# Every wait of TensorE as an instruction of its own, in a one-core transformer kernel of 14,410 matmuls

## The chip, the cores and the metric

The kernel runs on one core of a Trainium2 chip. The metric is the device time of one execution in microseconds (us). Three runs of the kernel before gave 2484.98, 2485.29 and 2485.33 us, so the median is 2485.29 us. A further execution was recorded by the hardware profiler; it took 2487.22 us, and all rows below come from it.

## The reference, cut to what matters

The program computes two transformer blocks in float32 on one sequence of 512 tokens with 1024 channels, one after the other.

```python
D_MODEL = 1024; SEQ = 512; D_FF = 2816; N_MEM = 256

def first_block(x, mem, ...):
    h = rmsnorm(x, norm_mix_pre)
    x = x + rmsnorm(parallel_mixer(h, ...), norm_mix_post)     # 31-tap conv branch, and 8-head attention
    h = rmsnorm(x, norm_mem_pre)
    x = x + rmsnorm(memory_cross_attention(h, ...), norm_mem_post)   # 4 heads of 256 over 256 memory rows
    h = rmsnorm(x, norm_ffn_pre)
    return x + rmsnorm(conv_gated_ffn(h, ...), norm_ffn_post)

def second_block(x, ...):
    for i in range(2):
        x = x + 0.5 * swiglu(rmsnorm_2(x, ffn1_norm[i]), ...)
        h = rmsnorm_2(x, mix_norm[i])
        x = x + (pool_mixer(h, ...) if i == 0 else mla_mixer(h, ...))
        x = x + 0.5 * swiglu(rmsnorm_2(x, ffn2_norm[i]), ...)
    return x

def swiglu(h, w_gate, w_up, w_down):
    return (silu(h @ w_gate) * (h @ w_up)) @ w_down
```

The matmuls of the five feed-forward parts are most of the work. The float32 result is wanted, so each product of two float32 matrices is made of three products in a shorter format, below.

## The kernel before, in words

All activations lie with their channels on the 128 partitions and the 512 tokens along the row. A weight matrix comes in units, most of them of 1024 rows and 128 columns. For each unit ScalarE writes a rounded copy `wh` (line 542) and VectorE the remainder `wl` (line 551); activations are split in the same way into `hxh` and `hxl` (lines 756 and 764) and other pairs. A product of the two matrices is then three matmuls for each block of 128 rows: high by high and the two mixed ones. They are lines 600, 601 and 602 in the helper `mm3`, and lines 1967 to 1969 in the four feed-forward parts that form sums of weight quarters and work on 256 tokens at a time. A unit of eight blocks is thus 24 matmuls into one PSUM bank, and a quarter unit of four blocks is 12.

In the program each matmul is one instruction, and it becomes two on the engine: a load of its 128 by 128 weights and the matmul proper. The profile shows the first as PEld and the second as PE. 
The order of the work on each engine is written out by hand, in functions with names such as `heads_tensor` or `block_tensor`. The engines meet through semaphores. Every engine has a wrapper class over `Engine`, whose method `wait_ge` (lines 185 to 189) takes a semaphore's name and a value. It does nothing when this engine has already waited for that value or a higher one (the dictionary `seen`), and otherwise issues a wait:

```python
        self.seen[kind] = value
        self.e.wait_ge(self.signals.sems[kind], value)
```

Of these some 650 have one or two waits more ahead of them, which makes 663 EVENT_SEMAPHORE instructions, of which 21 hold two waits. Together these are 1,993 waits.

The typical place is `linear`, which makes one tile of output:

```python
            e.wait_ge(*sig.at(("low", i)))
            for k in range(nk):
                sh, sl, ready = src(k0 + k)
                e.wait_ge(*sig.at(ready))
                made = mm3(e, o, (h[:, k, :], lo[:, k, :]), (sh, sl), first and k == 0, last and k == nk - 1)
```

It waits for the low part of the weight unit, and for each block of activations when that block is new. Its callers wait before that for the PSUM bank to be free. The last matmul of a tile raises `unit_done`.

The stages, by time in the profiled execution: the first block's projections and convolution until about 117 us, its attention (`main<-pt,vh` and `score<-kh,qh`, the latter with 64 active rows) until about 208 us, output projection and norm (about 280 to 305 us), attention over the memory (about 341 to 370 us), then the feed-forward parts, the pooling mixer near 1160 us and the latent attention (about 1900 to 2110 us).

Of the kernel before, what the change touches and what calls it, by code (L numbers as in the profile page):

```python
# [144 lines left out]
class Signals:  # L145

    def __init__(self, nc, ctx):
        self.nc, self.ctx = nc, ctx
        self.sems, self.count, self.table = {}, {}, {}  # L150
        self.final = False
# [26 lines left out]
class Engine:  # L178
# [6 lines left out]
    def wait_ge(self, kind, value):  # L185
        if self.e is None or kind is None or self.seen.get(kind, 0) >= value:
            return
        self.seen[kind] = value
        self.e.wait_ge(self.signals.sems[kind], value)
# [6 lines left out]
class Tensor(Engine):  # L196
    def __init__(self, signals, e):
        super().__init__(signals, e)
        self.matmul, self.transpose = (e.matmul, e.transpose) if e else (skip, skip)

class Scalar(Engine):
# [3190 lines left out]
```

## Time and profile before

| | before |
|---|---|
| median of three runs | 2485.29 us |
| lowest and highest | 2484.98 and 2485.33 us |
| the profiled execution's own time | 2487.22 us |
| its span, first to last instruction | 2485.9 us |
| outside the span | 1.3 us |
| granted TensorE clock, mean share of full speed | 0.996 |
| PE, PEld busy | 99%, 87% of the span |
| VectorE, ScalarE, GpSimd busy | 69%, 47%, 21% of the span |
| instructions recorded | 36,528 |

The times of matmuls overlap: one starts before the one ahead has left the engine. What a matmul costs in a stream is the distance from one start to the next, which is shorter than the duration in a row. "Releaser" is the instruction whose semaphore update ended a wait. In the chain of waits each piece is the work that the end of the execution was waiting for at that time, and "issue" is time between the release of an engine and the start of its instruction.

### The profile page before, as it was taken

What the parts mean: (1) busy time and instruction counts of PE and PEld (TensorE: products, weight loads), DVE (VectorE), ACT (ScalarE), POOL (GpSimd) and SP (SyncE); (2) the same over time, 40 slices, a digit from 0 to 9 for tenths busy, and PEclk for the clock granted to TensorE, in tenths of its full rate; (3) what the DMA queues carried; (4) which work ended last, traced back from release to release, by engine and by line L of the source; (5) the groups of instructions that cost most, each with busy time, mean ns of one, the idle gap of its engine ahead of it and who ended that gap; (6) DMA issues with size and microseconds to landing.
All of it is one profiled execution on the core that took longest, in us unless ns stands there. A gap on an engine that the chain in (4) does not pass through costs nothing.

```text
span 2485.9 us, 36528 instructions
## 1 busy us (share of the span) xinstructions
PE 2453.1 (99%) x14410; PEld 2155.1 (87%) x14410; DVE 1715.2 (69%) x2771; ACT 1173.4 (47%) x2028; POOL 514.0 (21%) x442
## 2 busy tenths in 40 slices
PE   9999999999999999999999999999999999999999
PEld 7767778888888989898889898989898888899998
DVE  6896655656634867677868677868677666776766
ACT  4485443444422635355635354535354554554543
POOL 4673302222201201002201002010101432201010
PEclk9999999999999999999999999999999999999999
DMA  5211312333232647452646454555542111456663
GB/s 174 79 43 60 94 51 68 102 93 100 83 102 81 157 134 172 134 149 88 157 135 171 135 149 123 149 145 161 143 121 84 49 52 52 131 153 147 159 146 101
DMA packets 110299, 287.57 MB, mean 116 GB/s; under 512 B 12080, under 2 KB 13616, under 8 KB 110128
## 3 DMA queue, kind: packets, MB, share of 16 engines
q1 hardware_dynamic: 88240, 245.37, 31.4%
q0 software_dynamic: 21888, 39.86, 10.2%
q8 instruction: 115, 1.88, 0.3%
q14 instruction: 56, 0.46, 0.1%
HBM read 283.08 MB, written 2.10 MB: 115 GB/s over the span
## 4 chain that ended last, share of the span: by engine, by line
PE 87%; DVE 7%; ACT 3%; issue 1%; POOL 1%; DMA 0%; SPq 0%; ACTq 0%; POOLq 0%; DVEq 0%
PE main L600 11%; PE main L602 10%; PE main L601 10%; PE score L600 6%; PE score L602 6%; PE score L601 6%; PE main L1969 4%; PE main L1968 4%; PE main L1967 4%; PE score L1967 4%; PE score L1969 4%; PE score L1968 4%; PE out L600 2%; PE out L1969 2%; PE out L1968 2%; PE out L1967 2%
## 5 line engine op out<-in xcount | busy, mean ns | idle before, releaser
L551 DVE TENSOR_TENSOR wl<-raw,wh 128x512 fp32r<-128x512 f32 (+2 forms) x507 | 495.0, 981 | 251.2 <-ACT wh L542 246.6
L542 ACT ACTIVATE wh<-raw 128x512 fp32r<-128x512 f32 (+2 forms) x507 | 415.8, 837 | 479.8 <-PE main L602 249.8
L507 POOL DMA_DIRECT2D sum<-in_wts x152 | 132.9, 903 | 954.7 <-DMA sum<-in_wts 943.6
L551 DVE TENSOR_TENSOR wl<-sum,wh 128x512 fp32r<-128x512 f32 x304 | 207.2, 687 | 62.8 <-ACT wh L542 57.1
L600 PE MATMUL main<-hxh,wh 128*128 128x512 f32 x616 | 242.7, 394 | 3.3 <-DVE hxl L764 1.8
L602 PE MATMUL main<-hxh,wl 128*128 128x512 f32 x616 | 240.1, 390 | 0.0
L601 PE MATMUL main<-hxl,wh 128*128 128x512 f32 x616 | 239.8, 389 | 0.0
L542 ACT ACTIVATE wh<-sum 128x512 fp32r<-128x512 f32 x304 | 177.2, 622 | 82.0 <-PE score L602 42.9
L672 POOL TENSOR_TENSOR acc<-acc,sq 128x512 f32<-128x512 f32 (+1 forms) x73 | 103.1, 1412 | 472.4 <-ACT sq L667 468.8
L1967 PE MATMUL score<-th,wh 128*128 128x256 f32 x548 | 155.4, 284 | 0.7 <-ACT kept L2071 0.5
L1969 PE MATMUL score<-th,wl 128*128 128x256 f32 x548 | 155.1, 283 | 0.0
L1968 PE MATMUL score<-tl,wh 128*128 128x256 f32 x548 | 155.1, 283 | 0.0
L600 PEld LDWEIGHTS main<-hxh,wh 128*128 128x128 f32 x616 | 115.7, 188 | 29.6 <-issue 2.3
L602 PEld LDWEIGHTS main<-hxh,wl 128*128 128x128 f32 x616 | 115.6, 188 | 24.4
L601 PEld LDWEIGHTS main<-hxl,wh 128*128 128x128 f32 x616 | 115.7, 188 | 23.1
L1968 PE MATMUL main<-hxl,wh 128*128 128x256 f32 x452 | 127.9, 283 | 0.0
L1969 PE MATMUL main<-hxh,wl 128*128 128x256 f32 x452 | 127.9, 283 | 0.0
L1967 PE MATMUL main<-hxh,wh 128*128 128x256 f32 x452 | 127.9, 283 | 0.0
L1969 PE MATMUL main<-th,wl 128*128 128x256 f32 x444 | 125.7, 283 | 0.0
L1968 PE MATMUL main<-tl,wh 128*128 128x256 f32 x444 | 125.7, 283 | 0.0
L1967 PE MATMUL main<-th,wh 128*128 128x256 f32 x444 | 125.6, 283 | 0.0
L2076 ACT ACTIVATE tmp<-tmp 128x512 f32<-128x512 f32 x88 | 55.5, 631 | 145.3 <-DVE tmp L2106 145.2
(517 smaller groups left out, 7099.2 us busy)
## 6 DMA issues: line engine op xcount, KB each, us to landing
raw<-in_wts SPq DMA_DIRECT2D x299, 512.0 KB, 3.6
sum<-in_wts SPq DMA_DIRECT2D x152, 256.0 KB, 2.9
sum<-in_wts POOLq DMA_DIRECT2D x152, 256.0 KB, 5.0
raw<-in_wts SPq DMA_DIRECT2D x80, 256.0 KB, 5.1
raw<-in_wts SPq DMA_DIRECT2D x52, 384.0 KB, 3.0
x<-in_xT SPq DMA_DIRECT2D x4, 512.0 KB, 7.4
out<-x SPq DMA_DIRECT2D x8, 256.0 KB, 2.0
memx<-in_memT SPq DMA_DIRECT2D x1, 1024.0 KB, 9.6
```

The source lines that it names most:

```text
L507: e.dma_start(t[:, :], stored(r + 1, part), accum_op=ALU.add).then_inc(*sig.up(("upper" if which == S3 else "gate") + f"_ended{n}", ("summ ...
L542: e.activation(halves_of(wh, i), src, ACT.Copy).then_inc(*sig.up("weight_high", ("high", i)))
L551: e.tensor_tensor(halves_of(wl, i), src, f(halves_of(wh, i)), ALU.subtract) \
L600: e.matmul(o, ah, bh, start=start, stop=False)
L601: e.matmul(o, ah, bl, start=False, stop=False)
L602: return e.matmul(o, al, bh, start=False, stop=stop)
L672: e.tensor_tensor(acc[:, 0:n], acc[:, 0:n], sq_turn(nm).of(("sq", nm, k))[:, 0:n], ALU.add) \
L1967: e.matmul(b[:, LEFT], h[:, k, :], mh, start=first and k == 0, stop=False, skip_group_check=not first)
L1968: e.matmul(b[:, LEFT], h[:, k, :], ml, start=False, stop=False, skip_group_check=not first)
L1969: made = e.matmul(b[:, LEFT], lo[:, k, :], mh, start=False, stop=k == 3, skip_group_check=not first)
L2076: e.activation(g[:, :], g[:, :], ACT.Silu, scale=-1.0 if (nm, c) in part_raw and c not in HALVED else 1.0) \
```

## The change

TensorE's wrapper gets a `wait_ge` of its own. It filters as before and issues the same wait, and then a no-operation instruction that must not be merged with what follows it. The wait rides on this instruction, so that no weight load carries one, and each wait stands apart. The other engines and the order of all work stay as they are.

```diff
@@ class Tensor(Engine)
         super().__init__(signals, e)
         self.matmul, self.transpose = (e.matmul, e.transpose) if e else (skip, skip)
+
+    def wait_ge(self, kind, value):
+        if self.e is None or kind is None or self.seen.get(kind, 0) >= value:
+            return
+        self.seen[kind] = value
+        self.e.wait_ge(self.signals.sems[kind], value)
+        self.e.nop(nofuse=True)
```

## Rows read from the trace of the kernel before

**Rows 1.** The page: busy time of engines, then the chain's shares by engine.

```profile
PE 2453.1 (99%) x14410; PEld 2155.1 (87%) x14410; DVE 1715.2 (69%) x2771; ACT 1173.4 (47%) x2028; POOL 514.0 (21%) x442
...
PE 87%; DVE 7%; ACT 3%; issue 1%; POOL 1%; DMA 0%; SPq 0%; ACTq 0%; POOLq 0%; DVEq 0%
```

**Rows 2.** Line 189's instructions on TensorE: count, duration ns, first and last start.

```profile
L189 PEldq EVENT_SEMAPHORE  x663: 51/51/4480, 6.4 to 2474.1; - x166
```

**Rows 3.** Waits of PEld, whole span: total us, times, longest us.

```profile
PEld main L600 <- issue: 12.2, 26, 1.2
PEld out L600 <- DVE hxl L764: 7.0, 7, 2.1
...
PEld turn L2907 <- DVE pm L2900: 0.3, 1, 0.3
```

**Rows 4.** Timeline of PEld across a tile's end (1002.43 us): start, duration.

```profile
1002.20 0.19 PEld L1969 LDWEIGHTS main<-th,wl 128*128 128x128 f32 x1
1002.32 0.19 PEld L1967 LDWEIGHTS score<-hxh,wh 128*128 128x128 f32 x1
1002.44 0.19 PEld L1968 LDWEIGHTS score<-hxl,wh 128*128 128x128 f32 x1
```

**Rows 5.** Timeline of PE across the same tile's end.

```profile
1002.20 0.28 PE L1968 MATMUL main<-tl,wh 128*128 128x256 f32 x1
1002.32 0.28 PE L1969 MATMUL main<-th,wl 128*128 128x256 f32 x1
1002.43 0.28 PE L1967 MATMUL score<-hxh,wh 128*128 128x256 f32 x1
```

**Rows 6.** Chain of waits, 180 us and 341 us: start, duration, what.

```profile
179.50 0.61 DVE pt L1312
180.10 0.04 issue
180.15 0.50 PE main L600
...
340.81 0.66 ACT pm L1728 x2
341.47 0.04 issue
341.51 0.39 PE score L600
```

**Rows 7.** Chain of waits, 305 us and 1189 us.

```profile
303.77 1.14 DVE wl L551
304.91 0.14 issue
305.05 0.47 PE score L600
...
1187.32 2.09 DVE wl L551
1189.41 0.14 issue
1189.55 0.47 PE main L600
```

**Rows 8.** Line 189 on TensorE, 423.60 to 423.85 us: first and last start.

```profile
L189 PEldq EVENT_SEMAPHORE  x2: 51/51/51, 423.7 to 423.8; - x2
```

**Rows 9.** Timeline of PEld, first attention: loads with 64 active rows.

```profile
138.28 0.18 PEld L600 LDWEIGHTS score<-kh,qh 64*128 64x128 f32 x1 [0.17 <-issue]
...
149.34 0.18 PEld L600 LDWEIGHTS score<-kh,qh 64*128 64x128 f32 x1 [0.17 <-issue]
```

**Rows 10.** Timeline, from 64 rows back to 128.

```profile
147.71 0.39 PE L602 MATMUL score<-kh,ql 64*128 64x512 f32 x1
...
148.02 0.19 PEld L600 LDWEIGHTS main<-pt,vh 128*128 128x128 f32 x1 [0.36 <-issue]
```

**Rows 11.** Timeline of PE in a stream of 512 columns.

```profile
303.20 0.39 PE L602 MATMUL out<-hxh,wl 128*128 128x512 f32 x1
303.43 0.40 PE L600 MATMUL main<-hxh,wh 128*128 128x512 f32 x1
303.66 0.39 PE L601 MATMUL main<-hxl,wh 128*128 128x512 f32 x1
```

## The prediction

> **What bounds the kernel now.** I read the page first. TensorE is busy for 99% of the span and makes 87% of the chain that ended last, against 7% for VectorE and 3% for ScalarE [rows 1]. So nearly every ns added to or taken from TensorE's stream shows in the time, and a change to other engines' waits would not.
>
> The timelines show how the stream runs. With 256 columns matmuls start 0.12 us apart [rows 5], with 512 columns 0.23 us [rows 11]. Each weight load starts together with the matmul ahead of it [rows 4, 5], so it lies under that matmul and costs nothing. At 1002.32 us in rows 4 the load is the first of a tile (`score<-hxh,wh` after `main<-th,wl`); there the code waits for its bank and its weights, one wait riding on the load. It starts no later than its neighbours, and the matmuls keep their 0.12 us. A wait whose semaphore has long been set is free in both forms: this kernel has both, 1,309 waits on loads and 663 standalone ones [rows 2], and steady stages show no gap at either.
>
> What is left is the list of waits and the chain. PEld sat idle until VectorE, ScalarE or GpSimd released it 74 times, 47.8 us in all (26 rows of the list, of which the first and the last stand here) [rows 3]. The chain comes back from another engine to TensorE 32 times. In 21 of these the piece between release and matmul is 0.04 us [rows 6]; in 11 it is 0.14 us [rows 7]. By the code the 21 are places where the late semaphore is the one on the load (`pt`, `pm`, `hxl`), and the 11 are places where the late one stands alone ahead of a load that carries another.
>
> **The change part by part.** All 1,993 waits become instructions of their own. 663 instructions go (21 held two waits) and 1,993 come, so 1,330 more for TensorE's sequencer.
>
> *A late wait that rode on a load.* It now costs what a late standalone one costs. From release to matmul start that is 0.14 instead of 0.04 us [rows 6, 7], +0.10. But the first matmul's piece of the chain is shorter behind a standalone wait, 0.47 against 0.50 us, because the load started 0.03 us ahead of it and not together with it. The second matmul is therefore later by 0.07 by the rounded rows, and I take 0.06 us, since 0.04 rounds up 0.042 in most such places.
>
> *A late wait that already stood alone.* It stays as it is, but the satisfied wait behind it, which rode on the load at no cost, is now one more instruction to get through. Two standalone waits directly in a row are recorded at 423.7 and 423.8 us with nothing late between them [rows 8], and again at 1175.9 and 1176.0 us: 0.1 us each. So +0.1 us.
>
> *The satisfied ones.* 1,330 more instructions at 0.1 us are 133 us of sequencer time in a span of 2485.9. They lie under matmuls as long as TensorE has queued work. Rows 5 leave room: a quarter unit of 12 matmuls takes 1.44 us and has two to four waits, 0.4 us. Where each block of a tile has its own wait, three matmuls of 512 columns take 0.68 us against two waits, 0.2 us. I cost them at nothing. If the cover is gone, just behind a late wait, one costs up to its 0.1 us; that is the upper end below.
>
> *The sum.* Lower bound, only what the chain shows: 21 x 0.06 + 11 x 0.1 = 1.3 + 1.1 = 2.4 us. It would be right if everything off the chain had slack. Upper bound, every late wait in full: 74 x 0.06 = 4.4, plus 22 standalone late ones in the trace (half of them on the chain, of which rows 7 are two) x 0.1 = 2.2, together 6.6, and 7.2 with a few satisfied waits uncovered. Successive late waits on one busy engine absorb each other: between 285 and 305 us VectorE makes `hxl` tile after tile and the chain comes to TensorE only at its end. Yet a chain names only one path, and at 99% busy a delay of TensorE off the chain mostly stays. I take 5.0 us, a little above the middle of 2.4 and 6.6. The profiled execution took 2487.22 us (span 2485.9 and 1.3 around it), so its successor would take 2492.2; it stands 1.9 us above the median of the runs, 2485.29, so the median goes to 2490.3 us, +0.20%.
>
> **A rule beside the rows.** Rows 6 and 7 show a release reaching a wait on a load in 0.04 us and a standalone one in 0.14. The Trainium skill, Perfetto Trace Analysis, section Tensor Engine Instruction, says that a load or matmul is pushed into a hardware wait queue and waits there while the sequencer already decodes the next one; its section Sequencer-only Instruction puts the wait of such an instruction in the sequencer itself. By that, after the change nothing behind an open wait is decoded, which agrees with the sign of the rows. It gives no price.
>
> No row shows a no-operation with a wait; EVENT_SEMAPHORE is the nearest, and I take its price. Both ends are kept for the range: nothing at all for each (0 us), and two instructions for each wait.
>
> **The rivals.**
>
> *Faster: a wait on a load keeps it from being moved under the matmul ahead.* The place would be the first attention. Loads with 64 active rows start only 0.17 us after the last load's end, on a semaphore long set [rows 9], and the load that goes back to 128 rows starts 0.31 us after the matmul ahead, not together with it [rows 10], where a stream has 0.23 [rows 11]. There are 32 switches each way. If the standalone form freed them, each would save about 0.09 us (0.20 against the 0.11 of the transposes ahead; 0.31 less 0.23, some 0.32 in others): 64 x 0.09 = 5.8 us, and less the 2.4 us at least of the late waits or more, some 2482 us. It decides if most of these 64 are due to the wait. Against it: the row at 138.28 us has no wait on its load by the code (seven of the 32 have none, since TensorE had waited for that value before), and it shows the same 0.17 us as the one at 149.34, which has one [rows 9]. So the number of rows seems to make the gap. The Trainium skill, TensorE: Matmul & The Clock Gate, Part 2, step 1, says that loads are pulled ahead of running matmuls where row groups don't conflict or the background buffer is used; it names no wait as a bar.
>
> *Dearer: each wait takes two instructions, or the no-operation is handled at twice the price.* Then a late wait on a load costs 0.06 + 0.1 = 0.16, and a late standalone one 0.3. On the chain 21 x 0.16 + 11 x 0.3 = 6.7; in full 74 x 0.16 + 22 x 0.3 = 18.4; the middle is 12.5, so 2497.8 us. For it: the code issues two calls. Against it: a wait normally rides on the next instruction, which is the no-operation.
>
> *Cheap: the no-operation passes faster than EVENT_SEMAPHORE, or what TensorE loses is slack.* Between 0 and 2.4 us; 2486.5 us. For it: the late waits of attention and norms sit in stretches where VectorE sets the pace.
>
> *The change doesn't do what it says:* the wait ends up on the load after all. Then 2485.3 us.
>
> **How the numbers follow.** This kernel's measurement can tell 0.2%, 5.0 us, from no change. The forecast has a chance of 0.63, with a range of its own of 2487.7 (lower bound) to 2492.5 (upper); it straddles the 0.2% mark at 2490.26, and I give 0.36 above it and 0.27 below. Dearer 0.13, cheap 0.13, no effect 0.05, faster 0.06. That makes slower 0.49, same 0.27 + 0.13 + 0.05 = 0.45, faster 0.06. The range is 2486.3 to 2498.5: it leaves out faster, no effect and the upper part of dearer.
>
> **What would show it.** In the profile after: some 1,990 no-operations on TensorE's sequencer and no EVENT_SEMAPHORE of line 189 (twice as many would be dearer). Chain pieces of 0.14 us or more before `main` and `score` L600 where rows 6 have 0.04, and about 0.25 where rows 7 have 0.14 (a satisfied wait behind the late one). The 0.12 and 0.23 us steps across tile ends unchanged, with the load still at its neighbour's start; if steps at tile ends grow, the cover that I cost at nothing is gone. Rows 9 and 10 unchanged; if their idle times vanish, the faster rival is right. A release-to-matmul time of 0.04 in the new form would make the sum wrong.

## The result, and the profile after

| | before | after |
|---|---|---|
| median of 12 runs | 2485.31 us | 2489.49 us |
| lowest and highest | 2484.50 and 2488.28 us | 2487.20 and 2492.71 us |
| profiled execution: time, span | 2487.22, 2485.9 us | 2492.35, 2491.0 us |
| granted clock in it | 0.996 | 0.995 |
| instructions recorded | 36,528 | 37,858 |

The changed kernel is slower by a little: ratio 1.0016, 95% interval [1.0008, 1.0023]. The change costs 4.2 us of the median, 5.0 were forecast, and 2489.49 us is 0.17% up, just inside the 0.2% that was called no change.

The page of the kernel after, section 1 and the chain's shares by engine:

```profile
PE 2454.5 (99%) x14410; PEld 2157.2 (87%) x14410; DVE 1715.5 (69%) x2771; ACT 1173.2 (47%) x2028; POOL 514.1 (21%) x442
...
PE 88%; DVE 7%; ACT 2%; issue 1%; POOL 1%; DMA 0%; SPq 0%; ACTq 0%; POOLq 0%; DVEq 0%
```

No engine's work has changed by more than 0.1% of the span [rows 1]. Line 206 is the new `wait_ge` of TensorE; here are its instructions, with duration in ns and first and last start:

```profile
L206 PEldq EVENT_SEMAPHORE  x1993: 51/51/51, 1.4 to 2479.3; - x200
```

There is one for each of the 1,993 waits, 1,330 more than before [rows 2]. The no-operation with a wait has become an EVENT_SEMAPHORE of the same 51 ns, so the price taken from such instructions is the right one, and the rival of two instructions for each wait is out.

The chain of waits after (start, duration, what), at the place of the first pair of [rows 6]:

```profile
180.34 0.61 DVE pt L1319
180.95 0.14 issue
181.09 0.47 PE main L607
```

and at the first place of [rows 7], then at two places where satisfied waits stand behind the late one, one of them at 1960 us and two at 2178 us:

```profile
304.86 1.14 DVE wl L558
306.00 0.14 issue
306.14 0.47 PE score L607
...
1959.43 0.76 DVE qn L2778
1960.19 0.25 issue
1960.44 0.47 PE main L607
...
2177.76 0.28 ACT kept L2078
2178.05 0.44 issue
2178.49 0.35 PE score L1974
```

The reader sees three things. A late wait that rode on a load went from 0.04 to 0.14 us, as forecast. The place at 305 us, where the late wait stood alone before, still has 0.14, not the 0.25 that I expected. And 0.25 or more appears elsewhere: at places where before the release took 0.04 us. The step from 0.14 to 0.25 is 0.11 us for one satisfied wait behind the late one. Two of them make 0.35 us, as at 846.26 us of the same chain; of the 0.44 at 2178.05 us some 0.09 us is more than that, and e2 has 0.35 at this place too, so this part comes and goes.

Steady stages are untouched. In PEld's timeline across the same tile's end as in [rows 4], now at 1005.79 us, the steps are 0.12 us all the way and no load starts late:

```profile
1005.67 0.19 PEld L1976 LDWEIGHTS main<-th,wl 128*128 128x128 f32 x1
1005.79 0.19 PEld L1974 LDWEIGHTS score<-hxh,wh 128*128 128x128 f32 x1
1005.91 0.19 PEld L1975 LDWEIGHTS score<-hxl,wh 128*128 128x128 f32 x1
```

The loads with 64 active rows keep their idle time too [rows 9], so the faster rival is wrong:

```profile
139.12 0.18 PEld L607 LDWEIGHTS score<-kh,qh 64*128 64x128 f32 x1 [0.17 <-issue]
...
150.18 0.18 PEld L607 LDWEIGHTS score<-kh,qh 64*128 64x128 f32 x1 [0.17 <-issue]
```

**The clock in single executions.** Each run lists its mean granted TensorE clock, and the time follows it in every kernel with enough runs: of the 61 runs of before in the experiments, 39 at 0.997 average 2484.61 us, 12 at 0.996 average 2487.12 and 5 at 0.995 average 2488.75, some 2.0 us for each 0.001. A 62nd run of before, 3432.68 us at a mean clock of 0.651, was in a slow state and is left out of all ratios and means. The clock falls to its lower level, 1.2 GHz, in a few short stretches, and where they lie differs from run to run. Two stretches by the view of stretches (length, busy us of PE, PEld, DVE, ACT and POOL with counts, granted clock, DMA share and GB/s), first of before:

```profile
1158.00:1163.00 5.00, 5.00 (x31) 5.00 (x31) 3.88 (x8) 3.53 (x9) 1.04 (x1) 0.66 0.01 2
290.00:297.00 7.00, 5.70 (x22) 3.58 (x21) 6.96 (x8) 3.54 (x6) 2.12 (x2) 1.00 0.26 77
```

and of after:

```profile
1158.00:1163.00 5.00, 5.00 (x46) 5.00 (x45) 2.85 (x5) 3.13 (x5) 1.04 (x1) 1.00 0.52 202
292.00:297.00 5.00, 4.62 (x13) 3.47 (x14) 4.96 (x7) 2.01 (x4) 1.71 (x1) 0.66 0.36 105
```

In the profiled execution of before the clock was low for part of the stretch from 1158 us, which after it was not, and the other way round from 292 us. So single profiles differ by some us for a reason that is not the change (these two lie 1.9 and 2.9 us above the medians of their kernels), and the experiments below are compared by medians and, beside them, by runs of equal granted clock.

### The profile page after: what moved, and what is told of

Same layout as the page of the kernel before. It is cut to its first block, busy times and chain, and to the rows that moved or that the text cites. A ratio compares the mean times of both kernels' runs of the same rounds, so it can differ in the third digit from the quotient of the medians.

```text
span 2491.0 us, 37858 instructions
## 1 busy us (share of the span) xinstructions
PE 2454.5 (99%) x14410; PEld 2157.2 (87%) x14410; DVE 1715.5 (69%) x2771; ACT 1173.2 (47%) x2028; POOL 514.1 (21%) x442
## 4 chain that ended last, share of the span: by engine, by line
PE 88%; DVE 7%; ACT 2%; issue 1%; POOL 1%; DMA 0%; SPq 0%; ACTq 0%; POOLq 0%; DVEq 0%
PE main L607 11%; PE main L608 10%; PE main L609 10%; PE score L607 6%; PE score L608 5%; PE score L609 5%; PE main L1976 4%; PE main L1975 4%; PE main L1974 4%; PE score L1974 4%; PE score L1976 4%; PE score L1975 4%; PE out L607 2%; PE out L609 2%; PE out L608 2%; PE out L1976 2%
```

## The experiments

A wait is called late when its semaphore is set only after TensorE has come to it, and satisfied when it was set before. Theory L, in the expectations, says that only late waits and what stands behind them cost time. Rival S says that the many satisfied waits cost, by filling TensorE's sequencer. Most kernels below are the kernel before with TensorE's waits gathered until the matmul that they precede, and then issued by a rule. A wait issued without the no-operation takes the old form: the first one issued rides on the load. Two tables hold the waits that were late in the profile of before: LATE_ON_LOAD the 74 on loads, LATE_ALONE 19 that stood alone. The diffs show only the lines that carry the rule of each kernel; the first is the helper that all of them share:

```diff
+    def wait(self, w, alone, times=1):
+        for _ in range(times):
+            self.e.wait_ge(self.signals.sems[w[0]], w[1])
+            if alone:
+                self.e.nop(nofuse=True)
```

| kernel | median us | runs | ratio to before, 95% | mean at clock 0.997, us (runs) | at 0.996 |
|---|---|---|---|---|---|
| before | 2485.42 (e1 to e4), 2485.24 (e5 to e7), 2485.88 (e8, e9) | 33, 17, 12 | | 2484.61 (39) | 2487.12 (12) |
| the change | 2489.49 | 12 | 1.0016 [1.0008, 1.0023] | 2488.75 (6) | 2490.68 (3) |
| e1 only the 74 late ones alone, last | 2487.24 | 11 | 1.0008 [0.9999, 1.0017] | 2487.10 (7) | 2487.75 (4) |
| e2 the same, in the code's order | 2489.83 | 11 | 1.0022 [1.0013, 1.0031] | 2488.32 (4) | 2490.59 (4) |
| e3 all the others alone | 2485.32 | 11 | 1.0000 [0.9991, 1.0008] | 2484.36 (6) | 2487.23 (4) |
| e4 late ones moved onto the load | 2486.10 | 11 | 0.9998 [0.9989, 1.0007] | 2483.45 (1) | 2485.53 (7) |
| e5 the change, each wait twice | 2497.39 | 5 | 1.0055 [1.0043, 1.0067] | 2497.30 (2) | 2501.77 (1) |
| e6 satisfied waits alone, 4 times | 2500.68 | 4 | 1.0061 [1.0048, 1.0074] | 2499.01 (1) | 2500.68 (2) |
| e6 satisfied waits alone, 8 times | 2685.59 | 2 | 1.0804 [1.0786, 1.0823] | | |
| e7 the change, late one last | 2488.35 | 12 | 1.0019 [1.0002, 1.0037] | 2487.44 (7) | 2489.85 (1) |
| e8 the 21 on the chain, 5 times | 2495.41 | 8 | 1.0034 [1.0022, 1.0047] | 2495.12 (1) | 2495.61 (6) |
| e9 the 53 off the chain, 5 times | 2499.17 | 5 | 1.0051 [1.0033, 1.0068] | | 2499.36 (4) |

A line fitted through all these runs but those of the eightfold kernel, with one slope over the clock and a level for each kernel, gives the levels over before in us: the change 4.1, e1 1.9, e2 3.7, e3 0.3, e4 -1.2, e7 3.0, each within 0.7, and e5 13.4, e6 four times 14.1, e8 8.7, e9 12.0, each within 1.1. They are called "at equal clock" below. They count as the edit's effect only if the edit doesn't move the clock itself, which no run tests.

**e1: only the 74 late waits.**

```diff
+        late = [w for w in waits if has(LATE_ON_LOAD, w)]
+        alone = bool(late)
+        for w in [w for w in waits if w not in late] + late:
+            self.wait(w, alone)
```

> Of the kernel before only the 74 waits that rode on a weight load and came late there become instructions of their own, each as the last one ahead of its load; the 1,235 other waits still ride. Theory L (late waits): each costs 0.06 us more, its release-to-matmul time goes from 0.04 to 0.14 us. With 21 of them on the chain that is +1.3 us, with all 74 in full +4.6; I expect +2 to +4 us, so 2487.3 to 2489.3. Rival S (the many satisfied waits fill TensorE's sequencer): these 74 are 5% of the added instructions, so under 0.3 us. Rival C (the clock): the time moves only with the granted clock, and the runs of this kernel and of the one before lie on one line of time over clock.

Measured: +1.9 us at equal clock, +1.8 by the medians, just under what I expected (2 to 4). The interval of the ratio just holds 1, so it is the comparison at equal clock that tells e1 from before. 76 of the 1,330 added instructions, 6%, make nearly half of the change's cost, so rival S is wrong for this half. The late waits on loads that its chain names have 0.14 us from release to matmul. 1.9 lies between 1.3 (the chain's 21) and 4.6 (all 74), and nearer the chain.

**e2: the same places, in the order of the code.**

```diff
+        alone = any(has(LATE_ON_LOAD, w) for w in waits)
+        for w in waits:
+            self.wait(w, alone)
```

> As the run before it, but the waits ahead of these 74 loads stand in the order of the code, as in the changed kernel: the late one first, and behind it 17 satisfied ones in 15 places. Theory L: another 0.11 us for each of the 17, 1.9 us in full and about 0.6 (5 of them on the chain) at least, so all of the change's +4.2 us: 2489 to 2490. Rival S: no different from the run before it and from the kernel before. In the profile the release-to-matmul time at 83 and 1957 us should be 0.25 us, not 0.14.

Measured: +3.7 us at equal clock, 1.8 more than e1 (within 0.9), for 17 instructions of 0.11 us, which is 1.9 in full. Against the change's +4.1 nothing that can be measured is left. The chain of waits at the same matmul in e1, where the satisfied wait comes ahead of the late one,

```profile
1955.89 0.76 DVE qn L2824
1956.65 0.14 issue
1956.79 0.47 PE main L245
```

and in e2, where it comes behind:

```profile
1955.55 0.76 DVE qn L2823
1956.31 0.25 issue
1956.56 0.70 PE main L245 x2
```

**e3: the complement.**

```diff
+        alone = not any(has(LATE_ON_LOAD, w) for w in waits)
+        for w in waits:
+            self.wait(w, alone)
```

> The complement: all waits become instructions of their own except those ahead of the 74 loads, 1,904 of the 1,993. Theory L: no change within 0.5 us, since all of them lie under queued matmuls, and the places where the late wait already stood alone have it last in either form. Rival S: most of the +4.2 us, so 2489 or more. If the 0.1 us behind a late standalone wait were paid as I had predicted (11 on the chain), +1.1 us at least.

Measured: 2485.32 against 2485.42 us, ratio 1.0000. The satisfied waits, 1,254 added instructions, cost nothing that can be measured (0.3 us within 0.7 at equal clock), and neither do the 19 places where the late wait stood alone already. At 1953.83 us its chain still has 0.04:

```profile
1953.03 0.76 DVE qn L2823
1953.79 0.04 issue
1953.83 0.50 PE main L245
```

**e4: the opposite direction.**

```diff
+        late = [w for w in waits if has(LATE_ALONE, w)]
+        for w in late + [w for w in waits if w not in late]:
+            self.wait(w, False)
```

> The opposite direction: the kernel before, with the late wait put on the weight load in the 19 places where it stood alone and a satisfied one rode. Theory L: 19 x 0.06 = 1.1 us less in full, 11 x 0.06 = 0.7 us less on the chain: 2484.2 to 2484.7. Release-to-matmul at 305 and 1189 us goes from 0.14 to 0.04 us. Rivals S and C: no change.

At equal clock -1.2 us, as theory L has it in full; the plain median is 0.7 us above before and the ratio's interval holds 1, so without the clock nothing would show. More of its runs fell to 0.996 and below (9 of 11, against 22 of the 61 of before). Whether that is chance or comes of the edit is not shown; if it comes of the edit, the gain is not there. What is shown is the step in the chain. Here it is at the first place of [rows 7]:

```profile
303.72 1.14 DVE wl L591
304.86 0.04 issue
304.90 0.96 PE score L233 x3
```

By the medians this version is no better than the kernel before, and 3.4 us better than the changed one.

**e5: each wait twice.**

```diff
+        for w in waits:
+            self.wait(w, True, 2)
```

> The changed kernel with each of its 1,993 waits issued twice, the same semaphore and value, so 3,986 instructions of their own. Theory L (only what stands at and behind a late wait costs, 0.11 us each): beside the changed kernel one more instruction behind each of the 74 + 19 late waits, and one more for each of the 17 satisfied ones behind them, 110 x 0.11 = 12.2 us in full. The 74 alone reached the end for two fifths of their price (1.9 of 4.6 us), the 17 wholly; by that 74 x 0.11 x 0.4 + 17 x 0.11 + 19 x 0.11 = 7.2 us over the changed kernel, 2496 to 2498 us. Rival S (satisfied waits cost wherever they are): twice the change's cost, +4.2 over it, 2493.6.

Measured: 2497.39 us, 7.9 over the changed kernel by the medians, inside theory L's 2496 to 2498 and outside rival S's 2493.6. At 0.997 alone it is 8.5 over it, and 9.4 by the fitted line. So doubling the instructions costs about twice what the change itself did. Theory L has the reason: a duplicate behind a late wait adds 0.11 us there, where the first only cost 0.06, and 110 of them are 12.2 us in full, of which 7.9 to 9.4 arrive.

**e6: satisfied waits four and eight times.**

```diff
+        late = any(has(LATE_ON_LOAD, w) or has(LATE_ALONE, w) for w in waits)
+        for w in waits:
+            self.wait(w, not late, 1 if late else 4)
```

> The kernel before, with each of the 1,866 or so waits that stand before a matmul without any late one issued four times, each time as an instruction of its own, so about 7,480; the places with a late wait keep their form. At 0.11 us each these are 830 us of sequencer time. Theory L with the cover of queued matmuls: a tile of 12 matmuls gives 1.44 us and its two or so waits now take 0.9, so only the dense places show: +3 to +12 us, about 2495. If there were no cover, +600 us.

> The same eight times, about 14,900 instructions, 1.66 ms of sequencer time. Two waits take 1.8 us and the tile's 12 matmuls 1.44, so here the cover is gone in the stages of quarter units and the sequencer sets the pace: +100 to +250 us. If the time stayed near the kernel before, an instruction of this kind would cost much less than the 0.11 us read from two in a row.

Measured: +15.4 us for four times, above the +3 to +12 I gave, and +200 us for eight times, inside it. Four times is 5,600 instructions more than e3, 0.62 ms of sequencer time at 0.11 us, of which 15 us reach the end; twice as many again is 0.83 ms more and 185 us reach it. The cover of queued matmuls is real, large, and has an end. The eightfold kernel's clock was lower too, 0.983 and 0.985; by the 2.0 us for each 0.001, far outside where that was read, my estimate is that some 26 of its 200 us are the clock's. Page of the eightfold kernel, section 1: TensorE's share fell from 99% to 95%.

```profile
PE 2557.9 (95%) x14410; PEld 2192.6 (82%) x14410; DVE 1725.6 (64%) x2771; ACT 1185.5 (44%) x2028; POOL 511.1 (19%) x442
```

**e7: the change, with the late wait last.**

```diff
+        late = [w for w in waits if has(LATE_ON_LOAD, w) or has(LATE_ALONE, w)]
+        for w in [w for w in waits if w not in late] + late:
+            self.wait(w, True)
```

> The changed kernel with one thing different: where several waits stand ahead of one matmul, the late one comes last (15 + 19 places, of which the 19 had it last already). Theory L: the 17 satisfied instructions behind a late wait go, -1.9 us: 2487.3 to 2487.8, as in the run in which the 74 alone were made instructions. Rival S: as the changed kernel, 2489.5.

Measured: 2488.35 us, 0.6 above the range of theory L and 1.1 below the changed kernel. At equal clock it is +3.0 over before, where e1 has +1.9 and e3 +0.3; it is 0.8 above their sum, within the 1.1 by which that difference is uncertain. Below the changed kernel it is by 1.0 within 0.9, where theory L has 1.9. The sign is that of theory L, and the size is not settled. Four of its 12 runs had a clock of 0.995 or less and lie at 2491 us and above, which is why its interval is wide.

**e8 and e9: the 21 on the chain and the 53 off it, five times each.**

```diff
+        late = [w for w in waits if has(PADDED, w)]
+        for w in [w for w in waits if w not in late]:
+            self.wait(w, bool(late))
+        for w in late:
+            self.wait(w, True, 5)
```

> The kernel before, with the 21 late waits on loads that the chain of waits names issued five times each, as instructions of their own and last ahead of their load: 0.06 + 4 x 0.11 = 0.51 us more for each, 10.7 us in all. If the chain names the waits that set the end, all of it arrives: 2494.5 to 2496.5. If the chain is no better than any other choice, the two fifths that all 74 together showed: +4.3, 2489.7.

> The same for the other 53 late waits on loads, which the chain does not name: 53 x 0.51 = 27 us in full. Theory of the lower bound (everything off the chain has slack): under 2 us, though half a us each may use the slack up. Theory of the upper bound: +27, 2512. Expected: between, since successive late waits on one busy engine absorb each other but a few stand near the chain: +8 to +16, 2493 to 2501.

Measured: +9.5 us for the 21 beside the runs of before taken with it (2485.88), of 10.7 in full, so 0.89 of each delay arrives; at equal clock +8.7, 0.81. The 53 off the chain give +13.3 of 27, a half, and +12.0 at equal clock, 0.44. Both medians lie inside what was expected. The chain of e8 at the place of [rows 6] has 0.56 us: 0.14 for the late wait and four repeats of it at 0.105 each, a little under the 0.11 between waits on different semaphores:

```profile
179.70 0.61 DVE pt L1355
180.30 0.56 issue
180.87 0.93 PE main L234 x3
```

## Why the prediction was right, step by step

*The bound.* Right. TensorE's share and all other engines' work are unchanged, and the delays at TensorE's waits add up to the difference (below).

*The satisfied waits at nothing.* Right, and shown by e3 (1.0000; 0.3 us within 0.7 at equal clock) and by the tile ends. The price of 0.1 us is right too: it is the 0.11 us step between 0.14 and 0.25 in the chains. What the prediction could not say is how thick the cover is; e6 shows it: four times is nearly covered, eight times is not.

*A late wait on a load, +0.06.* Right. 0.04 went to 0.14 us and the first matmul's piece from 0.50 to 0.47. All 74 together cost 1.9 us at equal clock (e1), where the sum had 1.3 to 4.4.

*A late wait that stood alone, +0.1 for the satisfied one behind it.* Wrong as to the place, and this is the step that failed. Its count of 11 also needs a word: the chain's view prints 0.14 us at 7 of the 11 only. At the other four, ahead of `main` L2608 at 1985, 2025, 2045 and 2065 us, it names VectorE's `qst` and prints 0.00 to 0.04 us; there the standalone wait was for ScalarE's `sq`, which ended 0.14 us before the matmul (at 1985.30 and 1985.44 us). I took the order of instructions for the order of the code. In the old form the first wait that the code issues before a matmul rides on the load, and so stands last; the later ones stand alone ahead of it. (The description ahead of the prediction, by which the last issued one rides, has this the wrong way round as far as the code is meant.) In the changed kernel they stand in the code's order. So where the late wait stood alone, it is now the last and nothing comes behind it: 0.14 us at 305 us before and after, cost nothing (e3). Where the late wait rode on a load and others stood ahead of it, 15 places, it is now the first, and 17 satisfied waits come behind it at 0.11 us each: 0.25 us at 1960, 0.35 at 846 and, with the 0.09 more, 0.44 at 2178. Together they cost 1.8 us (e2 less e1). The term that I had put elsewhere was 1.1 to 2.2 us, so this part of the sum came out right by luck: both sets happen to be of like size.

*How much of a late wait's delay arrives.* The choice of 5.0 in 2.4 to 7.2 was a little high. For small delays most waits off the chain have slack: 0.06 each gave 1.9 in all, and 21 x 0.06 = 1.3 of that is the chain's. With 0.51 each (e8, e9) the chain's waits passed on 0.8 to 0.9 of it and the others nearly a half. That a longer delay uses the slack up is my reading of it, which no run tests alone. The 17 instructions behind late waits passed on nearly all of their 1.9 us (e2 less e1); why they did and the 0.06 us ones did not is not shown by any run, and the difference of 1.8 is itself uncertain by 0.9.

*The whole.* 1.9 + 1.8 + 0.3 = 4.0 us (e1, e2 less e1, e3) against the 4.1 at equal clock and the 4.2 of the medians. The forecast of 5.0 was 0.8 too high, because less of the late waits' delay arrived (e1) than the choice in the middle had.

*The rivals.* Faster: wrong, the 64-row loads kept their 0.17 us with the wait taken off them, and the load back to 128 rows still starts 0.31 us after the matmul ahead (148.55 and 148.86 us after), as in [rows 10]. So the row count of the load is left as the cause that the rows allow, which no run here tests by itself. Dearer: wrong, one instruction each. Cheap: nearer than I gave it credit for, in that most off-chain waits cost little, but its range ended at 2.4 us. No effect: wrong.

*The rule of the Trainium skill.* Its split of waiting in a queue behind the sequencer and waiting in the sequencer (Perfetto Trace Analysis, sections Tensor Engine Instruction and Sequencer-only Instruction) agrees in sign with 0.04 against 0.14 us; the page has no price: no return of the chain to TensorE takes under 0.14 us after the change, and in e4, where every late wait rides, all 29 take 0.04.

## What to carry to other kernels

In this kernel a wait cost by whether it was late and by what stood behind it, and the number of satisfied ones mattered only once they outran the queued matmuls (e6). So list the waits that end late, and let the late one ride on the weight load, with the satisfied ones ahead of it as instructions of their own. In the program text of this kernel that means issuing the late one first, since the first issued rides. Here that was worth 1.2 us at equal clock and nothing by the medians (e4), so it is a small gain at best. And before single profiles are compared, compare their granted clocks: here 0.001 of it went with 2 us, half of what the change did.

## What the runs showed of the hardware that was not expected

One and the same program differs by 4 us between single executions, in step with the granted clock (2484.61 us at 0.997, 2488.75 at 0.995, before). A satisfied wait as an instruction of its own takes TensorE's sequencer 0.11 us though its record says 51 ns, and nearly all of that is hidden while matmuls are queued: 1,254 of them added nothing measurable (e3), some 5,600 more, 0.62 ms of sequencer time, added 15 us, and twice as many again 185 us (e6). The release of a wait on a weight load reaches the matmul in 0.04 us, that of a standalone one in 0.14 us, and each further one behind it adds 0.11 (0.105 where it repeats the same semaphore; once 0.20 at 2178 us of the changed kernel's trace).
